# A kernel of two transformer blocks: the queries' rotated features from 256 weight columns instead of 512, and other PSUM banks for the first two feed-forward chunks

## What is computed

```
def rope(x, positions):                      # last axis r = 32
    ang = positions * inv_freq               # 16 frequencies
    x1, x2 = x[..., :16], x[..., 16:]
    return concat([x1 * cos(ang) - x2 * sin(ang), x2 * cos(ang) + x1 * sin(ang)])

q = (rmsnorm(cq, q_norm_g) @ w_uq).reshape(b, s, 8, 64 + 32)
q_mla = concat([q[..., :64], rope(q[..., 64:])])
k_mla = concat([k_nope, broadcast(rope(k_rope)) to 8 heads])
logits = q_mla @ k_mla^T / sqrt(96), causal softmax, times v
...
h = modulate(rmsnorm(x, norm_ffn_g), shift, scale)
u = conv3(h @ w_up);  x = x + gate * ((silu(u[:, :2816]) * u[:, 2816:]) @ w_down)
```

## Time and profile before

| | before |
|---|---|
| median of 3 runs | 1001.64 us |
| the profiled execution | 1001.23 us |
| its span, first to last instruction | 999.1 us |
| TensorE busy (PE) | 989.2 us, 99% |
| TensorE weight loads (PEld) | 891.4 us, 89% |
| VectorE (DVE) | 719.1 us, 72% |
| ScalarE (ACT) | 597.8 us, 60% |
| bytes moved by DMA | 196.72 MB |
| mean granted TensorE clock | 0.999 of full speed |

### The profile page before, as it was taken

The page is one execution under the profiler, slowest core; times in us unless marked ns, Lnnn a source line. Parts: engine busy times, 40 slices in busy tenths (PEclk is TensorE's granted clock), DMA queues, the critical chain, the costliest instruction groups (busy, mean ns, idle before and its releaser), DMA issues.

```text
span 999.1 us, 16659 instructions
## 1 busy us (share of the span) xinstructions
PE 989.2 (99%) x6652; PEld 891.4 (89%) x6652; DVE 719.1 (72%) x1225; ACT 597.8 (60%) x1010; POOL 0.4 (0%) x5
## 2 busy tenths in 40 slices
PE   9999999999999999999999999999999999999997
PEld 8899999998888888999999888888999899888886
DVE  5898888878888988887658665655766558565652
ACT  4778666557566666767647545554665547455452
POOL 0000000000000000000000000000000000000000
PEclk9999999999999999999999999999999999999999
DMA  9975667535656664553326555555554327555521
GB/s 369 403 250 183 260 234 288 211 128 211 211 204 227 224 234 168 211 209 127 127 87 221 204 206 203 176 184 200 216 187 142 127 106 254 194 185 175 206 82 42
DMA packets 28443, 196.72 MB, mean 197 GB/s; under 512 B 3152, under 2 KB 3664, under 8 KB 5584
## 3 DMA queue, kind: packets, MB, share of 16 engines
q1 hardware_dynamic: 28224, 195.41, 54.7%
q10 hardware_dynamic: 144, 0.26, 0.1%
HBM read 194.61 MB, written 1.05 MB: 196 GB/s over the span
## 4 chain that ended last, share of the span: by engine, by line
PE 77%; DVE 13%; ACT 6%; issue 2%; DMA 1%; SPq 0%; DVEq 0%; ACTq 0%
PE PS L1382 16%; PE PS L1269 10%; PE PS L1069 8%; PE PS L1070 7%; PE PS L1071 7%; DVE wlo L1948 7%; PE PS L1273 5%; PE PS L1222 3%; PE PS L1225 3%; PE PS L1223 3%; ACT whi L1544 2%; PE PS L1303 2%; ACT PB L1832 2%; PE PS L1304 2%; PE PS L1305 2%
## 5 line engine op out<-in xcount | busy, mean ns | idle before, releaser
L1948 DVE TENSOR_TENSOR wlo<-raw,whi 128x1024 fp32r<-128x1024 f32 x306 | 358.3, 1216 | 60.5 <-ACT whi L1544 57.9
L1544 ACT ACTIVATE whi<-raw 128x1024 fp32r<-128x1024 f32 x300 | 297.8, 1047 | 58.8 <-PE PS L1382 53.2
L1269 PE MATMUL PS<-HX,whi 128*128 128x512 f32 x736 | 230.9, 395 | 1.5 <-issue 1.5
L1273 PEld LDWEIGHTS PS<-HX,wlo 128*128 128x128 f32 x736 | 138.3, 188 | 32.3
L1069 PE MATMUL PS<-HX,whi 128*128 128x256 f32 x496 | 145.1, 292 | 0.6 <-DVE HX L1922 0.5
L1273 PE MATMUL PS<-HX,wlo 128*128 128x256 f32 x736 | 144.6, 278 | 0.0
L1070 PE MATMUL PS<-HX,whi 128*128 128x256 f32 x496 | 140.2, 283 | 0.0
L1071 PE MATMUL PS<-HX,wlo 128*128 128x256 f32 x496 | 140.1, 282 | 0.0
L1269 PEld LDWEIGHTS PS<-HX,whi 128*128 128x128 f32 x736 | 114.5, 189 | 4.2 <-issue 1.7
L1069 PEld LDWEIGHTS PS<-HX,whi 128*128 128x128 f32 x496 | 94.8, 191 | 5.9 <-issue 4.3
L1070 PEld LDWEIGHTS PS<-HX,whi 128*128 128x128 f32 x496 | 95.0, 191 | 0.2
(11 more groups left out here) (276 smaller groups left out, 1817.0 us busy)
## 6 DMA issues: line engine op xcount, KB each, us to landing
raw<-wall SPq DMA_DIRECT2D x151, 1024.0 KB, 5.1
raw<-wada SPq DMA_DIRECT2D x18, 1024.0 KB, 5.0
raw<-wall SPq DMA_DIRECT2D x8, 512.0 KB, 16.8
GA<-wada SPq DMA_DIRECT2D x2, 1024.0 KB, 21.6
GA<-alibi SPq DMA_DIRECT2D x1, 2048.0 KB, 9.4
raw<-wall SPq DMA_DIRECT2D x2, 768.0 KB, 6.2
X<-xt SPq DMA_DIRECT2D x1, 1024.0 KB, 5.0
KM<-wada SPq DMA_DIRECT2D x1, 1024.0 KB, 14.4
```

The source lines that it names most:

```text
L1269: e.matmul(PS[:, b + nt, :], whi[place(n)][:, at + nt * 128:at + nt * 128 + 128], HX[:, k, :, :].rearrange("p h t -> p (h t)"), start=k == ...
L1273: m = e.matmul(PS[:, b + nt, 0:T], wlo[place(n)][:, at + nt * 128:at + nt * 128 + 128], Hh[:, k, :], start=False, stop=k == 7, skip_group_ ...
L1544: e.activation(whi[place(n)][:, c], raw[i % RAW][:, c], ACT.Copy).then_inc(*up("a_whi", (n, half)))
L1948: e.tensor_tensor(wlo[place(n)][:, c], raw[i % RAW][:, c], f32(whi[place(n)][:, c]), ALU.subtract).then_inc(*up("v_wlo", (n, half)))
```

## The change

The second halves of the rotated features are no longer a second set of matmul outputs. Chunk `("uq", 1)` has now 256 output columns (all heads' first halves of 16, then all heads' second halves), 768 columns in all, split in halves of 512 and 256. Its matmuls are one pair of tiles in one bank. VectorE makes four products' worth in two instructions from that bank, then the difference and the sum. ScalarE copies the first halves to `QM[64:96]`, and VectorE, in the new step `copy_second`, the second halves to `QM[96:128]`, in four instructions each; every source of 32 partitions (two heads) goes to two heads, and the key has zeros in the places of the other head, by the columns "even" and "odd". The step `signs` is gone, `turn_key` has four instructions, `copy_key` two. The MLA scores contract all 128 partitions. `copy_second` is a chore: it comes one `refill` after `copy_rope`, behind the split of `("in", 10)` and ahead of that of `("in", 11)`. Before the first two feed-forward chunks the bank counter is set to 2. Since the rotated features take one bank fewer, every bank handed out by `bank()` between them and that point is one earlier in the turn than before.

```
-USED = {"uq": 1536}
+USED = {("uq", 0): 1536, ("uq", 1): 768}
+HALF = {("uq", 1): 512}
...
-            emit("signs")
...
     def ev_uq_rope(n, b, pr):
-        emit("ev_uq_rope", n, b, pr)
-        if pr == 1:
-            chores.append(lambda: emit("copy_rope"))
+        emit("ev_uq_rope", n, b)
+        chores.extend([lambda: emit("copy_rope"), lambda: emit("copy_second")])
...
-    rows(("uq", 1), "lat", pairs=2, mid=False, evac=ev_uq_rope)
+    rows(("uq", 1), "lat", mid=False, evac=ev_uq_rope)
...
+            st["at"] = 2
             together([("up", 0), ("up", 1)], "ffn", ev_first)

             st["at"] += st["at"] % 2
...
     def half_cols(n, half):
-        return slice(half * CH // 2, min(USED.get(ORDER[n][0], CH), (half + 1) * CH // 2))
+        cut = HALF.get(ORDER[n], CH // 2)
+        return slice(half * cut, min(USED.get(ORDER[n], CH), (half + 1) * cut))
...
+                if ORDER[n] == ("uq", 1):
+                    ncols = 256
...
-                free[a[1]] = ("v_qr", a[2])
+                free[a[1]] = ("v_qr", "parts")
...
-                        q, k = QM[0:96, h, :], KM[0:96, h, :]
+                        q, k = QM[:, h, :], KM[:, h, :]
...
+                        on.wait_ge("v_qr", "copied")
...
             elif step == "copy_key":
                 on.wait_ge("v_kr", "turned")
-                e.activation(
-                    KM[64:96, :, :], V[64:96, 0, 256:512].unsqueeze(1).to_broadcast([32, 8, T]), ACT.Copy).then_inc(
-                    *up("a_kr", 0))
+                for h0, mask in ((0, "even"), (1, "odd")):
+                    m = e.activation(
+                        KM[64:128, h0:8:2, :], V[64:128, 0, 256:512].unsqueeze(1).to_broadcast([64, 4, T]), ACT.Identity,
+                        scale=col(mask, 0, 1, 64, 128))
+                m.then_inc(*up("a_kr", 0))
             elif step == "copy_rope":
                 on.wait_ge("v_qr", "sum")
                 for j in range(4):
-                    m = e.activation(QM[64:96, j:8:4, :], TT[32 * j:32 * j + 32, :, :], ACT.Copy)
+                    m = e.activation(
+                        QM[64:96, 2 * j:2 * j + 2, :], TT[32 * j:32 * j + 32, 0, :].unsqueeze(1).to_broadcast([32, 2, T]), ACT.Copy)
...
-            elif step == "signs":
-                on.wait_ge("a_sin", 1)
-                e.tensor_scalar(SIN[:, :], SIN[:, :], col("sgn"), None, ALU.mult).then_inc(*up("v_rope", "signs"))
...
             elif step == "turn_key":
-                k0, k1 = V[64:96, 0, 256:512], V[64:96, 1, 256:512]
+                k0, k1 = V[64:128, 0, 256:512], V[:, 1, 256:512]
...
-                e.tensor_tensor(k0, FK[64:96, :], COS[64:96, :], ALU.mult)
-                e.tensor_tensor(k1, FK[96:128, :], SIN[96:128, :], ALU.mult).then_inc(*up("v_kr", "parts"))
+                e.tensor_tensor(k0, FK[64:128, :], COS[64:128, :], ALU.mult)
+                e.scalar_tensor_tensor(k1[64:96], FK[96:128, :], -1.0, SIN[96:128, :], ALU.mult, ALU.mult)
+                e.tensor_tensor(k1[96:128], FK[64:96, :], SIN[64:96, :], ALU.mult).then_inc(*up("v_kr", "parts"))
...
             elif step == "ev_uq_rope":
-                n, b, pr = a
-                dst, table = ((TT[:, :, :], COS), (SQ[:, 0:2, :], SIN))[pr]
-                on.wait_ge("t_mm", (n, pr))
...
-                e.tensor_tensor(dst, two(b), table[:, :].unsqueeze(1).to_broadcast([128, 2, T]), ALU.mult).then_inc(
-                    *up("v_qr", pr))
-                if pr == 1:
-                    on.wait_ge("v_qr", 1)
-                    e.tensor_tensor(TT[:, :, :], TT[:, :, :], SQ[:, 0:2, :], ALU.add).then_inc(*up("v_qr", "sum"))
-                    tt_free[0] = tt_free[1] = ("a_qr", 0)
+                cosines, sines = (x[:, :].unsqueeze(1).to_broadcast([128, 2, T]) for x in (COS, SIN))
+                e.tensor_tensor(TT[:, :, :], two(b), cosines, ALU.mult)
+                e.tensor_tensor(SQ[:, 0:2, :], two(b), sines, ALU.mult).then_inc(*up("v_qr", "parts"))
+                on.wait_ge("v_qr", "parts")
+                e.tensor_tensor(TT[:, 0, :], TT[:, 0, :], SQ[:, 1, :], ALU.subtract)
+                e.tensor_tensor(TT[:, 1, :], TT[:, 1, :], SQ[:, 0, :], ALU.add).then_inc(*up("v_qr", "sum"))
+                tt_free[0] = tt_free[1] = ("a_qr", 0)
+            elif step == "copy_second":
+                on.wait_ge("v_qr", "sum")
+                for j in range(4):
+                    m = e.tensor_copy(
+                        QM[96:128, 2 * j:2 * j + 2, :], TT[32 * j:32 * j + 32, 1, :].unsqueeze(1).to_broadcast([32, 2, T]))
+                m.then_inc(*up("v_qr", "copied"))
```

More of the change, by code:

```diff
@@ L43, in _columns @@
         ("q_norm_g", 3), ("kv_norm_g", 2), ("conv_w", 132), ("conv_b", 44), ("attn_norm", 16),
-        ("mlp_norm", 16), ("subln", 1), ("b_forget", 1), ("invf", 1), ("sgn", 1),
+        ("mlp_norm", 16), ("subln", 1), ("b_forget", 1), ("invf", 1), ("even", 1), ("odd", 1),
         ("eps", 1), ("m1", 8), ("m2", 8), ("m3", 1), ("m4", 1), ("id", 128),
@@ L978, in half_cols, with half_with @@
     def half_cols(n, half):
-        return slice(half * CH // 2, min(USED.get(ORDER[n][0], CH), (half + 1) * CH // 2))
+        cut = HALF.get(ORDER[n], CH // 2)
+        return slice(half * cut, min(USED.get(ORDER[n], CH), (half + 1) * cut))
+    def half_with(n, last):
+        return (last - 1) // HALF.get(ORDER[n], CH // 2)
     STEPS = stages()
@@ L1000, in load @@
             else:
-                n = USED.get(it[2], CH)
+                n = USED.get(it[2:4], CH)
                 e.dma_start(raw[slot][:, 0:n], wall[it[1]][:, 0:n]).then_inc(*up(f"d_raw{slot}", i, 16))
@@ L1060, in weights_there @@
                 return
-            on.wait_ge(hi_mark(n), (n, (last - 1) // (CH // 2)))
-            on.wait_ge("v_wlo", (n, (last - 1) // (CH // 2)))
+            on.wait_ge(hi_mark(n), (n, half_with(n, last)))
+            on.wait_ge("v_wlo", (n, half_with(n, last)))
         def split_there(key):
@@ L1928, in trig_there @@
         def trig_there():
-            on.wait_ge("a_sin", 0)
-            on.wait_ge("v_rope", "signs")
+            on.wait_ge("a_sin", 1)
         for step, *a in STEPS:
@@ L2203, in vector @@
             elif step == "turn_key":
-                k0, k1 = V[64:96, 0, 256:512], V[64:96, 1, 256:512]
+                k0, k1 = V[64:128, 0, 256:512], V[:, 1, 256:512]
                 on.wait_ge("a_ev", (FIRST, 1))
                 trig_there()
-                e.tensor_tensor(k0, FK[64:96, :], COS[64:96, :], ALU.mult)
-                e.tensor_tensor(k1, FK[96:128, :], SIN[96:128, :], ALU.mult).then_inc(*up("v_kr", "parts"))
+                e.tensor_tensor(k0, FK[64:128, :], COS[64:128, :], ALU.mult)
+                e.scalar_tensor_tensor(k1[64:96], FK[96:128, :], -1.0, SIN[96:128, :], ALU.mult, ALU.mult)
+                e.tensor_tensor(k1[96:128], FK[64:96, :], SIN[64:96, :], ALU.mult).then_inc(*up("v_kr", "parts"))
                 on.wait_ge("v_kr", "parts")
-                e.tensor_tensor(k0, k0, k1, ALU.add).then_inc(*up("v_kr", "turned"))
+                e.tensor_tensor(k0, k0, k1[64:128], ALU.add).then_inc(*up("v_kr", "turned"))
             elif step == "ev_uq_rope":
-                n, b, pr = a
-                dst, table = ((TT[:, :, :], COS), (SQ[:, 0:2, :], SIN))[pr]
-                on.wait_ge("t_mm", (n, pr))
+                n, b = a
+                on.wait_ge("t_mm", (n, 0))
                 trig_there()
@@ L2469, in _chunks @@
     cq, ckv, kr, fq, fk, fv, ff, gm, gf = (r(cut[i], cut[i + 1]) for i in range(9))
-    sw = np.concatenate([r(16, 32), r(16)])
-    cols_in = np.concatenate([cq, np.tile(ff, 8), kr, kr[sw], ckv, fk, fq, fv, gm, gf])
-    uq = np.concatenate([p + 96 * h for p in (r(64), 64 + r(32), 64 + sw) for h in range(8)])
+    kr1, kr2 = kr[0:16], kr[16:32]
+    cols_in = np.concatenate([cq, np.tile(ff, 8), kr1, kr1, kr2, kr2, ckv, fk, fq, fv, gm, gf])
+    uq = np.concatenate([p + 96 * h for p in (r(64), 64 + r(16), 80 + r(16)) for h in range(8)])
     ukv = np.concatenate([np.concatenate([r(64) + 128 * h for h in range(8)]),
@@ L2483, in _chunks @@
         elif kind == "uq":
-            t = np.pad(_tiles(a["w_uq"][0], uq[512 * i:512 * i + 512]), ((0, 0), (0, 512)))
+            t = _tiles(a["w_uq"][0], uq[512 * i:512 * i + 512])
+            t = np.pad(t, ((0, 0), (0, 2048 - t.shape[1])))
         elif kind == "ukv":
@@ L2527, in _smalls @@
         np.tile(a["b_forget"][0], 16)[:, None], inv[p % 16][:, None].astype(np.float32),
-        one(lambda q: -1.0 if q % 32 < 16 else 1.0), one(lambda q: EPS), m1, m2,
+        one(lambda q: 1.0 if q % 32 < 16 else 0.0), one(lambda q: 0.0 if q % 32 < 16 else 1.0), one(lambda q: EPS), m1, m2,
         one(lambda q: -8.0 if q >= 8 else 0.0), one(lambda q: 1.0 if q < 8 else 0.0),
```

## The result

The changed kernel takes **1009.60 us** (median of four runs, 1009.10 to 1010.85), the kernel before 1001.59 beside it: ratio 1.0081, 95% interval 1.0069 to 1.0094. It is slower by 8.0 us, where I had forecast +1.5 and a range up to 1005.3. The profiled execution took 1010.85 us with a span of 1008.7, which is 9.6 above the span of before (999.1).

What follows compares the result with a forecast made beforehand. It took TensorE, busy 99% of the span, to bound the kernel. Its terms, -1.5 (rotation) + 2.8 (feed-forward banks) + 0.2 (second block), summed to +1.5, so 1003.1 us against the median, range 1001.5 to 1005.3.

Steps and rivals of the forecast that it cites:

- Part 1: Rotated features' matmuls, from 78.69 us: 18 of 36 go, 0.120 us each, -2.2 us for TensorE.
- Part 2: VectorE up to the copies: smaller casts and low parts, so it ends the rotation 0.7 us earlier.
- Part 3: Four `copy_second` copies on VectorE among the splits: 1.35 us (1.3 to 2.5), leaving VectorE 0.65 us later.
- Part 4: Third MLA pair's transposes, slack 2.1 us: 0.7 comes back as waits, so TensorE keeps 1.5 of 2.2 us.
- Part 5, added: Feed-forward chunk 1 waits for the row's bank near 217 us: a TensorE gap of 4.5 us.
- Part 5, removed: TensorE's 1.7 us gap ahead of the first wide chunk, near 228 us, goes; with the added wait +2.8 net.
- Part 6: Second block, MoBA layer: the first wide chunk waits for the second evacuation instead of the first, +0.2 us.
- A: Rival: TensorE's clock falls in the new 4.5 us gap for 3 us, costing 1.3 us: 1004.4; chance 0.34.
- C: Rival: the copies take 2.5 us instead of 1.35: 1004.3; chance 0.11 together with E, without A.
- E: Rival: the wait at the banks is moved, not removed: up to +1.7 us; chance 0.11 with C, without A.

Runs made afterwards that it cites:

- e9: e1 with VectorE's four copies moved ahead of the scaling of fox pair 1: 1000.64 us (0.9992 of the kernel before).
- e6: e1 with ScalarE's evacuation of chunk ("in", 10) put ahead of the last fox pair's exponentials: 1002.59 us (1.0006 of the kernel before).
- e1: The changed kernel without the line that sets the bank counter to 2: 1002.66 us (1.0017 of the kernel before).
- e2: The rotation part of the change alone, with every bank as in the kernel before: 1002.41 us (1.0008 of the kernel before).
- e3: The kernel before with only the bank counter set to 2 ahead of the first feed-forward chunks: 1001.55 us (1.0000 of the kernel before).
- e7: e1 with the four copies of the second halves on ScalarE instead of VectorE: 1005.14 us (1.0033 of the kernel before).
- e4: e3 with the second feed-forward chunk's first part made to wait for the eighth scaled tile: 1008.07 us (1.0064 of the kernel before).
- e5: The changed kernel with 17 spare matmuls ahead of the second feed-forward chunk's waiting first part: 1008.35 us (1.0064 of the kernel before).

## Why the prediction was wrong

**Part 1, right.** TensorE is 2.1 us ahead at the transposes of 85.89 us.

**Part 2, right but for a tenth or two.** VectorE ends the rotation 0.5 us earlier (87.37 instead of 87.88), I had said 0.7.

**Part 3, a size too small.** The four copies take 1.73 us together, inside the bounds of 1.3 and 2.5, but I took 1.35, by a cast of the same columns. The rows of after:

```profile
98.28 1.22 DVE L1959 TENSOR_TENSOR wlo<-raw,whi 128x1024 fp32r<-128x1024 f32 x1
99.53 1.73 DVE L2236 COPY QM<-TT 32x512 f32<-32x512 f32 x4
101.29 1.23 DVE L1959 TENSOR_TENSOR wlo<-raw,whi 128x1024 fp32r<-128x1024 f32 x1
```

VectorE is 1.3 us late instead of 0.65. In e9, where the same four stand 8 us earlier, it is 0.2 late.

**Part 4 is the step that failed first.** I wrote "The tightest is the third MLA pair", with a slack of 2.1. The slack was well read: in e6, where VectorE is 1.85 late, TensorE's lead of 1.0 shrinks to 0.39 there, 2.2 in all. But it is not the tightest. Chunk `("in", 11)` waits for its bank with a slack of 0 (ScalarE's evacuation ended 0.05 us ahead of it before), and the third column sum with one of 0.8. I had searched for TensorE's waits among the probabilities that it transposes, and not gone through the banks that each chunk writes again. Nor does idle time show such a place: TensorE reached it just in time. So of 2.2 us not 1.5 stayed but -1.5 in the profiled executions of e1 and e2, and -0.9 by e2's median: by the latter the rotation part is wrong by 2.4 us, of which some 0.6 are VectorE's larger lateness (part 3) and the rest is this step.

**Part 5, added: right.** 4.34 us of idle time, forecast 4.5, at the place and ended by the instruction that I named.

**Part 5, removed: right as a gap, wrong as a gain.** 1.7 us of TensorE's idle time went, and e3 shows that they are worth nothing: TensorE is not what the feed-forward part waits for. My sentence on VectorE and ScalarE, that they fall 1.7 us more behind and that this is covered, looked for the next transfer or split and missed that their chain is the one that ends last. Here the busy shares of the earlier trace rows misled: TensorE is 99% busy, and for 175 us of that it is not on the path. The Trainium skill (Perfetto Trace Analysis, Identifying the Most-Contended Engine and Optimization Strategy) says to take the engine with the highest occupancy and to look for the gaps on it, within the regime of interest; for TensorE it warns that matmul busy time is no measure of how close it is to its limit, and points to the share of peak work done (MFU) and to the busy time of the weight loads. The trace agrees with the warning: from 228 to 403 us the matmuls are busy for 173.5 us, the weight loads for 148.7 and VectorE for 150.9, so that VectorE is level with TensorE there. By the matmuls' share alone one takes TensorE, as I did, and closing its gap gave 0.0 us (e3).

**Part 6, no cost to be seen.** e1, with all banks one earlier, and e3, with those of before, have the same 772 us behind the first reading of chunk 0. In the MoBA layer the first wide chunk starts 1.10 us behind the start of the evacuations (842.02 and 840.92 us), against 1.11 before, where I had added 0.2.

**The rivals.** A was right in kind, and I had it at 0.34. The clock fell, but for 6.8 us instead of 3, since I took its length from the start of the kernel; there gives a granted clock of 1.00, so that the row does not show the slow pace to be the lower clock. It costs 2.3 to 2.6 us, not 1.3. The executions say this of the gaps met here: 1.7 us, never a fall (e2); 2.5 us, in the profiled execution of after, and by the mean clock in four of eleven (e1); 2.6 us, in the profiled one of e7; 4.3 and 4.4 us, by the mean clock (0.995 or 0.996) in all four runs of after and all five of e4. The Trainium skill (TensorE: Matmul & The Clock Gate, The HAM clock gate) says that an idle engine is put back to 1.2 GHz and must work for a while to leave it, and the trace agrees: 0.51 granted over 3.5 and 7 us. C was right in that the copies were slower. E, that the wait is moved and not removed, was right for its 1.7 us, at a place 175 us away where I had not looked.

**The sum.** For the profiled execution, against before, in us: rotation part +1.5; the clock's fall at 117 us +1.2 (2.7 instead of e1's 1.5); the wait for the row +4.4; the clock's fall behind it +2.5 (what is left of the whole, inside 2.3 to 2.6); the gap closed 0.0. Together 9.6, the difference of the spans. By the medians the forecast of +1.5 was 6.5 us too low: 2.4 in the rotation part, 1.7 for the gap whose closing gave nothing, and some 2.4 for the clock behind the wait, which I had left to rival A. The other three runs have spans of 1007.0 to 1007.4 and a higher mean clock (0.996 instead of 0.995): most likely the first fall is missing in them, which would make it 8.1 to 8.4, and their spans are 7.9 to 8.3 above that of before; but no trace of theirs shows it.

**What stays open.** Where e9's gain of 1.0 us by the medians arises. Its profile cannot tell: its span is 999.1 us where the median of its runs is 998.7, and that of before is 999.1 where the runs beside e9 have 999.5. Why the clock holds or falls behind one and the same 2.5 us.

## What to carry to other kernels

Before a gain on the busiest engine is counted, find for each stretch the engine that waits for nobody: list the waits of all the others there. If VectorE's list names only ScalarE, and its busy time and these waits fill the stretch, then their loop sets the pace, however full TensorE looks, and the only useful date is when the loop starts. Slack is to be read at every place where the engine can wait, banks that are written again among them, and it can be zero where no idle time is shown. And work that must go onto a shared engine costs what its place in the order makes it cost: with the same 1.73 us of copies VectorE was 1.3 us late in one place and 0.2 in the other, and ScalarE's evacuation brought ahead helped only while VectorE was late.

## What the runs showed of the hardware

A copy of 32x512 from one SBUF tile to another partition range takes 0.43 us on VectorE and 0.64 on ScalarE, in a row of four (1.73 and 2.55 us): VectorE's is as long as a cast of 128x512 (412 ns), so that a quarter of the partitions saved nothing here. A gap of 4.4 us on TensorE cost half as much again, by the clock behind it (2.3 to 2.6 us, e4), and matmuls that nobody reads kept the clock at 1.00 (e5). With a gap of 2.5 us the runs of e1 fall into two groups some 2 us apart, most likely by the clock. A fall can come when the matmuls already run again: 1.4 us later in the profiled execution of after.
